# A fused two-block transformer on one core: each merge step carries an attention step, and seven stand between group norm steps

## The chip, the cores and the metric

The kernel runs on one core of a Trainium2 chip. The metric is the device time of one execution in microseconds (us), as the median of several runs. The engines are PE (TensorE, the matrix engine), DVE (VectorE), ACT (ScalarE), POOL (GpSimd) and SP (SyncE, which here issues the DMAs).

## The reference

Two transformer blocks on 256 tokens of width 1024, all in float32. Only block one matters here:

```python
def first_block(x, p, ...):
    u = rmsnorm(h, mix_pre_norm[i])
    z = u @ w_in[i]                                   # attention, RWKV and gate columns
    o_attn = dilated_attention_branch(z_attn)         # 4 heads, 3 dilation groups, 2 blocks of 128 queries
    o_rwkv = rwkv7_time_mix(z_rwkv, ...)              # 8 heads, a recurrence over the tokens, then group norm
    gate_attn, gate_rwkv = jnp.split(jax.nn.sigmoid(z_gate), 2, axis=-1)
    merged = gate_attn * (o_attn @ w_attn_up[i]) + gate_rwkv * (o_rwkv @ w_rwkv_up[i])
    h = h + rmsnorm(merged @ w_out[i], mix_post_norm[i])
    ...                                               # a feed-forward part and a gated embedding
```

Block two (three more attentions, an attention to a memory, a gated feed-forward part and the last norm) follows and is computed from `h`.

## The kernel before

Weights stream from DRAM through six slots of 1 MB. Each product with them is done in pieces (`parts` in the rows): a weight is split into a high part (ACT, a copy) and a low part (DVE, L2422), and PE multiplies high by high, high by low and low by high (L691, L692, L693).

The work is written as five programs, one for each engine, and all five walk through the same list of steps. A step is what stands between two `yield`s of a Python generator; the object `turns` says which generator gives the next step. Since an engine works its instructions off in the order in which they are written, the order of the steps is the order on every engine, and semaphores make one engine wait for another.

In the stretch of this case two generators are mixed (`turns.mix(fills(), rwkv(), order_1())`, L1309):

- "m", the fills. First the products for queries, keys and values, `qkv()`. Then the merge products (`gates()`: the 2048 gate columns of `w_in`, 4 ranges of 512 columns, 8 steps each, so 32 steps; a step is 6 matmuls of 128x512, called a gate step here) and `attention()` (24 steps). For each block of 128 queries i (0 or 1) and each pair of heads hh (0 or 1) the attention has 6 steps on PE: scores (L1231), nothing, transposes of one head (L697), transposes of the other (L697), nothing, values (L1274). In the first step DVE masks the scores of one head and takes their minimum (L2758), waits for ACT's exponential (L1694), inverts the sum (L2761) and scales (L2368, called the end of that head's softmax); in the second step it does the other head. For i=0 a head has 384 columns, for i=1 768. Then come the products with `w_attn_up` (two steps here, the rest later).
- "s", RWKV. For each chunk of 128 tokens i: products of keys and receptances, `first()` (L1053, L1068, L1081; DVE masks them at L2670 to L2673, L2678 and L2685), and `chain()`, six levels of a matrix inversion. A level is a step T (PE L1105 and L1108, then DVE masks the result, L2695, two instructions) and a step X (PE L1121 to L1129, then ACT copies it). After them come S (L1140; DVE copies it, L2701), X21 (L1150), the right side (L1171), u (L1185) and y (L1196 to L1201). `normed(i)` is the group norm of y: ACT copies y, DVE means and subtracts (L2640 to L2644), ACT squares, DVE sums (L2648), POOL takes the root (L3332), DVE scales (L2654), PE transposes (L697), ACT and DVE finish. The norm of chunk 0 runs beside the chain of chunk 1, the norm of chunk 1 after y. Then the four products with `w_rwkv_up` (L1288), beside which `w_out`'s first two slots are split.

How m and s alternate is a string written by hand, and how gates and attention alternate another:

```python
return itertools.chain("msmsm" * 12, "msmsmsm" * 16, "mmsmmsmsmsmsms", itertools.cycle("ms"))   # L532
yield from turns.alternate(gates(), attention(), "aab")                                          # L1304
```

With "aab" two gate steps are followed by one attention step; when the gates are at an end, the last 8 attention steps stand alone. Results go to 8 banks of PSUM. The attention takes banks 2, 3 and 4 in turn, RWKV banks 4, 5, 6 and 7, the gates banks 0 and 1: bank 4 has two owners. Before PE writes a bank again it waits until the engine that reads it has done so (`bank()`, which waits for the events in `free`).

Of the kernel before, what the change touches and what calls it, by code (L numbers as in the profile page):

```python
# [274 lines left out]
def program(nc, A, consts, vecs, pt, out):  # L275
    with ExitStack() as ctx:
# [54 lines left out]
        def const(off, n):  # L331
            return low[:, OC + off:OC + off + n]
# [196 lines left out]
              "wo2": (A["w_out_2"][0], [P + 26152, P + 28200, P + 19968, P + 17920], m2Hi, m2Lo)}  # L529

        def order_1():
            return itertools.chain("msmsm" * 12, "msmsmsm" * 16, "mmsmmsmsmsmsms", itertools.cycle("ms"))  # L532

# [142 lines left out]
        def tensor_program(e, turns):  # L678
# [4 lines left out]
            def bank(b):  # L683
                for event in free[b]:
                    q.wait_ge(*event)
                return PSUM[:, b, :]
# [254 lines left out]
            def gate(r, late):  # L941
                yield from token_range(st1, GATE_AT[r], 2, 512, lambda i: [main_act.at("g1", r, i)], late)

            def gates():
                for r in (2, 3, 0, 1):
                    yield from gate(r, (lambda: rotate("qk", 5, 2, rz1[1])) if r == 2 else nothing)
# [270 lines left out]
                yield from up("r", lambda k: ("rwkv_up", k), 4, o_rwkv, wait_rwkv, lambda i, n: [up_dve.at("r", i, n)], rw_bank)  # L1217

            def attention():
                for i in range(2):  # L1220
                    for hh in range(2):
                        W = 128 * (i + 1)
                        nb = 3 * (i + 1)
                        bs = [next(pa) for _ in range(i + 2)]
                        for b in bs:
                            bank(b)
                        q.wait_ge(*rope_dve.at("qk", 5, "sum"))

                        def score(par, g, b, o):
                            half = half_rows[par]  # L1230
                            return mm(PSUM[:, bs[b], o:o + W], qk[half, 2 * g + hh, 128 * i:128 * i + 128], qk[half, 6 + 2 * g + hh, 0:W], True, True)  # L1231

                        if i == 0:
                            for g in range(3):
                                for par in range(2):
                                    t = score(par, g, par, 128 * g)
                                    if g == 2:
                                        t.then_inc(at_pe.up("s", i, hh, par), 1)
                            for par in range(2):
                                free[bs[par]] = [at_dve.at("r", i, hh, par, 0)]  # L1240
                        else:
                            score(0, 2, 1, 0).then_inc(at_pe.up("shared", hh), 1)
                            for n in range(2):
                                t = score(0, n, 0, 256 * n)
                                if n == 1:
                                    t.then_inc(at_pe.up("s", i, hh, 0), 1)
                                score(1, 1 + n, 2, 256 * n)
                            q.wait_ge(*at_pe.at("shared", hh))
                            score(1, 0, 1, 256).then_inc(at_pe.up("s", i, hh, 1), 1)
                            for b, event in zip(bs, ((0, 0), (1, 0), (1, 1))):  # L1250
                                free[b] = [at_dve.at("r", i, hh, *event)]
                        yield
                        yield
                        for par in range(2):
                            q.wait_ge(*at_dve.at("e", i, hh, par))
                            for b0 in range(0, nb, 4):
                                k = min(4, nb - b0)
                                b = next(pa)
                                p = bank(b)
                                for j in range(k):  # L1260
                                    t = tr(p[:, 128 * j:128 * j + 128], at_sm[par][:, 128 * (b0 + j):128 * (b0 + j) + 128])
                                t.then_inc(at_pe.up("t", i, hh, par, b0), 1)
                                free[b] = [at_act.at("t", i, hh, par, b0)]
                            yield
                        yield
                        b = next(pa)
                        p = bank(b)
                        q.wait_ge(*main_act.at("v", 1, 1))
                        q.wait_ge(*at_act.at("t", i, hh, 1, 4 if nb > 4 else 0))
                        for n in range(nb):  # L1270
                            g, j = n // (i + 1), n % (i + 1)
                            for par in range(2):
                                h = 2 * hh + par
                                t = mm(p[half_rows[par], 0:128], vtok[:, j, 64 * (4 * g + h):64 * (4 * g + h) + 64],  # L1274
                                       at_eT[par][:, 128 * n:128 * n + 128], n == 0, n == nb - 1)
                        t.then_inc(at_pe.up("o", i, hh), 1)
                        free[b] = [at_act.at("o", i, hh)]
                        yield
# [22 lines left out]

            def fills():
                yield from qkv()
                yield from turns.alternate(gates(), attention(), "aab")  # L1304
                for _ in range(2):
                    turns.go("up", ups)
                    yield
# [376 lines left out]
        def scalar_program(e, turns):  # L1684
# [3 lines left out]
            def bank(b):  # L1688
                return PSUM[:, b, :]
# [172 lines left out]
            def gates():  # L1862
                for r in (2, 3, 0, 1):
                    yield from gate(r)
# [124 lines left out]
                yield from rwkv_up()  # L1989

            def attention():
                for i in range(2):
                    for hh in range(2):
                        W, nb = 128 * (i + 1), 3 * (i + 1)
                        for _ in range(i + 2):
                            next(pa)
                        for par in range(2):
                            q.wait_ge(*at_dve.at("r", i, hh, par, i))
                            s = at_sm[par][:, 0:3 * W]
                            act(s, s, ACT.Exp, scale=-1.0, bias=sm_at[par][0][:, i:i + 1], accum=sm_at[par][1]) \  # L2000
                                .then_inc(at_act.up("x", i, hh, par), 1)
                            yield
                        for par in range(2):
                            for b0 in range(0, nb, 4):
                                k = min(4, nb - b0)
                                p = bank(next(pa))
                                q.wait_ge(*at_pe.at("t", i, hh, par, b0))
                                copy(at_eT[par][:, 128 * b0:128 * (b0 + k)], p[:, 0:128 * k]).then_inc(at_act.up("t", i, hh, par, b0), 1)
                            yield
                        yield  # L2010
                        p = bank(next(pa))
                        q.wait_ge(*at_pe.at("o", i, hh))
                        copy(o_attn[:, hh, 128 * i:128 * i + 128], p[:, 0:128]).then_inc(at_act.up("o", i, hh), 1)
                        yield
# [15 lines left out]

            def fills():
                yield from qkv()
                yield from turns.alternate(gates(), attention(), "aab")
                for _ in range(2):
                    turns.go("up", ups)
                    yield
# [321 lines left out]
        def vector_program(e, turns):  # L2358
# [184 lines left out]
            def gates():  # L2543
                for r in (2, 3, 0, 1):
                    yield from gate(r, (lambda: rotate1(5)) if r == 2 else nothing)
# [189 lines left out]

            def attention():
                ma = const(C_MA, 768)
                for i in range(2):
                    for hh in range(2):
                        W, nb = 128 * (i + 1), 3 * (i + 1)  # L2740
# [53 lines left out]

            def fills():
                yield from qkv()
                yield from turns.alternate(gates(), attention(), "aab")
                for _ in range(2):
                    turns.go("up", ups)
                    yield  # L2800
# [427 lines left out]
        def gpsimd_program(e, turns):  # L3228
# [46 lines left out]
            def steps(n):  # L3275
                for _ in range(n):
                    yield
# [31 lines left out]
            def gates():  # L3309
                for r in (2, 3, 0, 1):  # L3310
                    yield from gate(r, nothing)
# [34 lines left out]
                yield from steps(4)  # L3346

            def attention():
                yield from steps(24)

            ups = steps(4)

            def fills():
                yield from qkv()
                yield from turns.alternate(gates(), attention(), "aab")
                for _ in range(2):
                    turns.go("up", ups)
                    yield
# [194 lines left out]
```

## Time and profile before

| | us |
|---|---|
| median of three runs | 983.81 (983.28 to 984.82) |
| the profiled execution, its own time | 984.61 |
| its span in the trace | 982.5 |
| PE busy in the span | 939.3 (96%) |
| DVE busy | 578.5 (59%) |
| ACT busy | 426.5 (43%) |
| mean granted clock of PE | 0.995 of full speed |

Times in rows are microseconds from the start of the span; "busy" of PE is modelled, since its matmuls are pipelined, so the time from the start of one piece to the start of the next is the better measure of a piece. The stretch of this case goes from 156 to 286 us. The masking instruction of the attention is called CUSTOM_DVE_ANT in the trace and ISA in the order of the program.

### The profile page before, as it was taken

To read this page: it belongs to the slowest core of one execution; us is meant where nothing else is said; L and a number is where in the kernel's file an instruction comes from. 1 tells how busy PE (TensorE), PEld (TensorE's weight loads), DVE (VectorE), ACT (ScalarE), POOL (GpSimd) and SP (SyncE) were. 2 spreads that over 40 slices of the span, in tenths; PEclk is the share of its full clock that TensorE was granted. 3 is DMA by queue.
4 is the path that set the end of the run, shared out by engine and by line. 5 is a ranking of instruction groups with operands and counts; after the bars stand their busy time and mean duration, and the time that the engine had idled before them with its cause. 6 is when DMAs were issued, how large, how long until landed. Compare 5 with 4: busy or idle time off the path is not lost.

```text
span 982.5 us, 15768 instructions
## 1 busy us (share of the span) xinstructions
PE 939.3 (96%) x6794; PEld 773.5 (79%) x6794; DVE 578.5 (59%) x903; ACT 426.5 (43%) x679; POOL 46.9 (5%) x62
## 2 busy tenths in 40 slices
PE   5999999989989999999999999989999899999996
PEld 3998888767558988888879988765568698888885
DVE  1569765744463566655764567853672456667672
ACT  2574334333342344455543446462430344455560
POOL 1010000100000000000000450000000000000000
PEclk9999999999999999999999999999999999999999
DMA  9345242221545865555438684323555457675531
GB/s 330 116 129 172 89 129 87 88 79 58 209 159 165 248 178 190 195 183 203 128 129 191 137 239 139 128 87 111 191 169 150 117 157 197 173 192 194 177 123 43
DMA packets 134948, 151.83 MB, mean 155 GB/s; under 512 B 15936, under 2 KB 106304, under 8 KB 134752
## 3 DMA queue, kind: packets, MB, share of 16 engines
q1 hardware_dynamic: 133952, 147.14, 48.5%
q10 hardware_dynamic: 928, 3.70, 1.0%
q8 instruction: 53, 0.87, 0.4%
q14 instruction: 15, 0.12, 0.0%
HBM read 149.78 MB, written 1.05 MB: 154 GB/s over the span
## 4 chain that ended last, share of the span: by engine, by line
PE 85%; DVE 7%; ACT 4%; issue 2%; DMA 1%; POOL 0%; POOLq 0%; SPq 0%; ACTq 0%; DVEq 0%
PE psum L802 10%; PE psum L691 8%; PE psum L693 8%; PE psum L692 8%; PE psum L754 7%; PE psum L803 6%; PE psum L774 4%; PE psum L1288 4%; PE psum L775 3%; PE psum L783 3%; PE psum L697 2%; PE psum L860 2%; PE psum L850 2%; PE psum L851 2%; PE psum L805 1%
## 5 line engine op out<-in xcount | busy, mean ns | idle before, releaser
L1697 ACT ACTIVATE parts<-low 128x1024 fp32r<-128x1024 f32 (+2 forms) x234 | 236.9, 1047 | 107.0 <-PE psum L693 64.1
L2422 DVE TENSOR_TENSOR parts<-low,parts 128x1024 fp32r<-128x1024 f32 (+2 forms) x148 | 181.1, 1251 | 39.7 <-ACT parts L1697 39.2
L691 PE MATMUL psum<-parts 128*128 128x512 f32 (+2 forms) x424 | 170.9, 403 | 2.7 <-DVE parts L2422 2.7
L693 PE MATMUL psum<-parts 128*128 128x512 f32 (+2 forms) x424 | 164.1, 387 | 0.0
L692 PE MATMUL psum<-parts 128*128 128x512 f32 (+2 forms) x424 | 163.8, 386 | 0.0
L802 PE MATMUL psum<-parts 128*128 128x512 f32 x434 | 155.7, 398 | 0.0
L1697 ACT ACTIVATE high<-psum 128x512 f32<-128x512 f32 (+5 forms) x103 | 56.5, 566 | 184.3 <-PE psum L805 73.0
L803 PE MATMUL psum<-parts 128*128 128x256 f32 x496 | 129.1, 281 | 0.0
L691 PEld LDWEIGHTS psum<-parts 128*128 128x128 f32 x424 | 79.8, 188 | 23.5 <-DVE parts L2422 4.9
L803 PEld LDWEIGHTS psum<-parts 128*128 128x128 f32 x496 | 93.6, 189 | 5.7
L802 PEld LDWEIGHTS psum<-parts 128*128 128x128 f32 x434 | 81.7, 188 | 16.9
L693 PEld LDWEIGHTS psum<-parts 128*128 128x128 f32 x424 | 79.8, 188 | 16.3
L692 PEld LDWEIGHTS psum<-parts 128*128 128x128 f32 x424 | 79.9, 188 | 15.2 <-issue 1.2
L2482 DVE TENSOR_TENSOR parts<-low,parts 128x1024 fp32r<-128x1024 f32 x54 | 66.0, 1222 | 35.3 <-ACT parts L1697 35.3
L774 PE MATMUL psum<-parts 128*128 128x256 f32 x280 | 74.3, 300 | 2.1 <-ACT parts L1697 2.1
L754 PE MATMUL psum<-low 128*128 128x128 f32 (+2 forms) x640 | 73.3, 275 | 2.4 <-DVE low L2399 2.4
L754 PEld LDWEIGHTS psum<-low 128*128 128x128 f32 (+2 forms) x640 | 71.9, 188 | 3.8 <-DVE low L2399 3.3
L775 PE MATMUL psum<-parts 128*128 128x256 f32 x280 | 69.3, 282 | 0.0
L774 PEld LDWEIGHTS psum<-parts 128*128 128x128 f32 x280 | 53.4, 191 | 6.5 <-issue 5.3
L775 PEld LDWEIGHTS psum<-parts 128*128 128x128 f32 x280 | 53.5, 191 | 1.3 <-issue 1.2
L2837 DVE TENSOR_TENSOR mid<-psum,high 128x512 f32<-128x512 f32 x31 | 21.4, 692 | 44.7 <-ACT high L1697 44.7
L3236 POOL TENSOR_TENSOR low<-low 128x1 f32<-128x1 f32 x20 | 11.0, 552 | 676.6 <-DVE low L2368 676.6
(304 smaller groups left out, 1330.9 us busy)
## 6 DMA issues: line engine op xcount, KB each, us to landing
low<-in_w_in_dram SPq DMA_DIRECT2D x40, 1024.0 KB, 5.2
low<-in_w_ffn_in_dram SPq DMA_DIRECT2D x44, 512.0 KB, 5.1
low<-in_w_ff_in_dram SPq DMA_DIRECT2D x16, 1024.0 KB, 5.8
low<-in_w_ff_out_dram SPq DMA_DIRECT2D x16, 1024.0 KB, 4.9
low<-in_w_ffn_out_dram SPq DMA_DIRECT2D x11, 1024.0 KB, 5.0
low<-in_w_out_dram SPq DMA_DIRECT2D x8, 1024.0 KB, 6.0
low<-in_w_ple_gate_dram SPq DMA_DIRECT2D x4, 1024.0 KB, 5.0
low<-in_w_up_dram SPq DMA_DIRECT2D x3, 1024.0 KB, 5.0
```

The source lines that it names most:

```text
L691: mm(o, l[0], r[0], start, False)
L692: mm(o, l[0], r[1], False, False)
L693: return mm(o, l[1], r[0], False, stop)
L754: t = mm(PSUM[0:m, banks[n], 256 * j + 128 * i:256 * j + 128 * i + 128], w3[:, k, off:off + m], uT[:, k, 128 * i:128 * i + 128], k == 0, k ...
L774: mm(o, hi[:, k, c], st.uh[:, k, :], k == 0, False)
L775: mm(o, lo_[:, k, c], st.uh[:, k, :], False, False)
L802: mm(p, hi[:, k, c], st.u2(k), k == 0, False)
L803: mm(p[:, 0:256], lo_[:, k, c], st.uh[:, k, :], False, False)
L1288: t = mm(p, l[:, k, 128 * i:128 * i + 128], slot(held(*key(k // 2)))[:, 1024 * (k % 2) + 512 * n:1024 * (k % 2) + 512 * n + 512], k == 0, ...
L1697: return e.activation(o, a, ACT.Copy)
L2422: tt(rslot3(n, nk, width)[:, r, 0:w], slot3(n, nk, width)[:, r, 0:w], st.hi3(j)[:, r, 0:w].bitcast(F32), ALU.subtract) \
L2482: tt(rview(OR + 2048 * n + 1024 * (k % 2), 1024), slot(n)[:, 1024 * (k % 2):1024 * (k % 2) + 1024], rview(base, 1024).bitcast(F32), ALU.su ...
```

## The change

Three things are changed, in all engine programs alike. `attention()` starts with an empty step, so it has 25. Gates and attention are no longer alternated by "aab" but paired: each m step is one gate step followed in the same step by one attention step, so that after 25 of the 32 steps the attention is at an end and seven gate steps are left. And the string of `order_1` is another: from the sixth group on it is written out, with one s between m and m nearly everywhere, twice two in a row ("mssmss"), and "sssss" at the end of the group norm.

```diff
-            return itertools.chain("msmsm" * 12, "msmsmsm" * 16, "mmsmmsmsmsmsms", itertools.cycle("ms"))
+            return itertools.chain("msmsm" * 12, "msmsmsm" * 5, "ms" * 7, "mssmss", "ms" * 23, "sssss", itertools.cycle("ms"))
@@ def attention(): (in each engine's program; POOL's has steps(25) for steps(24))
+                yield
                 for i in range(2):
                     for hh in range(2):
@@ def fills(): (in each engine's program)
                 yield from qkv()
-                yield from turns.alternate(gates(), attention(), "aab")
+                yield from turns.paired(gates(), attention())
                 for _ in range(2):
                     turns.go("up", ups)
                     yield
```

`turns.paired(a, b)` stands in the kernel already: each of its steps is a step of a and then one of b, while both last.

No instruction is added or removed on any engine; lines behind the new ones are two or three higher (DVE's L2695 is L2697 there, L2758 is L2761, L2422 is L2424; PE's L1288 is L1289). Three places show what moves.

The first is DVE in the third level of chunk 1's chain, before. L2758 to L2368 are one head of the attention for i=0 (384 columns), the two L2695 the masks of a step T, L2422 a split of the gate weights:

```order
L2758 ISA mid,low<-psum,low 128x384
L2758 ISA low 128x1
L2761 RECIPROCAL low<-low 128x1
L2368 TENSOR_SCALAR mid<-mid,low 128x384
L2695 TENSOR_TENSOR high<-psum,low 64x512 x2
L2422 TENSOR_TENSOR parts<-low,parts 128x1024
```

And the same place on DVE in the changed kernel (L2761 and L2764 are the attention, L2697 the masks, L2424 the split):

```order
L2761 ISA mid,low<-psum,low 128x512
L2761 ISA low 128x1
L2761 ISA mid,low<-psum,low 128x256
L2761 ISA low 128x1
L2764 RECIPROCAL low<-low 128x1
L2370 TENSOR_SCALAR mid<-mid,low 128x768
L2697 TENSOR_TENSOR high<-psum,low 64x512 x2
L2424 TENSOR_TENSOR parts<-low,parts 128x1024
L2761 ISA mid,low<-psum,low 128x256
```

The head ahead of the masks is now one of i=1, with 768 columns in two pieces, and the next head's first piece stands right behind the split. In the sixth level the same stands once more, without the split.

The second is DVE at the start of chunk 1, in the changed kernel: masks of the key products (L2672 to L2675, the last three rows of six are shown), the mean of the group norm, the masks L2680 and L2687, with an attention head between them:

```order
L2675 TENSOR_TENSOR high<-high,low 128x4x64
L2642 TENSOR_REDUCE low<-high 128x8
L2370 TENSOR_SCALAR low<-low 128x8
L2646 TENSOR_TENSOR high<-high,low 128x512
L2680 TENSOR_TENSOR high<-psum,low 128x4x128 x2
L2761 ISA mid,low<-psum,low 128x384
L2761 ISA low 128x1
L2764 RECIPROCAL low<-low 128x1
L2370 TENSOR_SCALAR mid<-mid,low 128x384
L2687 TENSOR_TENSOR high<-psum,low 128x512 x2
```

Before, L2685 (the same as L2687) followed L2678 (L2680) at once, and no attention head stood ahead of the six masks either.

The third is PE at the end of the stretch, before: L1288 are the products with `w_rwkv_up` and `w_attn_up`, L1231, L697 and L1274 the attention's scores, transposes and values:

```order
L697 MATMUL psum<-low,mid 128x128 x6
L1288 MATMUL psum<-low,high 128x512 x4
L1274 MATMUL psum<-mid 64x128 x12
L1288 MATMUL psum<-low,high 128x512 x4
L1231 MATMUL psum<-mid 128x256 x6
L1288 MATMUL psum<-low,high 128x512 x8
L697 MATMUL psum<-low,mid 128x128 x12
L1274 MATMUL psum<-mid 64x128 x12
L1288 MATMUL psum<-low,high 128x512 x8
L697 MATMUL psum<-low,high 128x128 x8
```

The same place on PE in the changed kernel, from the last gate matmul on:

```order
L693 MATMUL psum<-parts 128x512
L697 MATMUL psum<-low,high 128x128 x4
L1289 MATMUL psum<-low,high 128x512 x24
L697 MATMUL psum<-low,high 128x128 x8
L850 MATMUL psum<-parts 128x512
```

The attention is gone from there: all of it stands between gate steps and RWKV's steps, up to the step u of chunk 1. Between y and the transposes of the group norm stand six gate steps and nothing else.

## Rows read from the trace of the kernel before

**Rows 1.** The page, the chain that ended last, by engine:

```profile
PE 85%; DVE 7%; ACT 4%; issue 2%; DMA 1%; POOL 0%; POOLq 0%; SPq 0%; ACTq 0%; DVEq 0%
```

**Rows 2.** Waits of PE, 155 to 290 us: total, times, longest:

```profile
PE psum L1121 <- DVE high L2695: 3.2, 4, 1.1
PE psum L697 <- DVE mid L2368: 2.0, 1, 2.0
PE psum L1105 <- ACT high L1697: 1.0, 1, 1.0
PE psum L697 <- ACT mid L1697: 0.9, 1, 0.9
PE psum L1274 <- DVE high L2371: 0.8, 1, 0.8
PE psum L697 <- DVE high L2654: 0.8, 1, 0.8
PE psum L1274 <- ACT mid L1697: 0.7, 1, 0.7
PE psum L1288 <- issue: 0.4, 1, 0.4
```

**Rows 3.** Timeline of PE, end of the stretch: start, length, work, idle before:

```profile
256.56 1.53 PE L1274 MATMUL psum<-mid 128*64 128x128 f32 x24 [0.78 <-DVE high L2371]
...
275.70 2.83 PE L1274 MATMUL psum<-mid 128*64 128x128 f32 x24 [0.69 <-ACT mid L1697]
```

**Rows 4.** Windows: busy of PE, PEld, DVE, ACT, POOL, granted clock, DMA, GB/s:

```profile
275.00:276.00 1.00, 0.31 (x5) 0.33 (x6) 0.86 (x1) 0.56 (x2) 0.00 (x0) 0.72 0.99 408
...
647.00:648.00 1.00, 1.00 (x4) 0.80 (x5) 1.00 (x7) 1.00 (x3) 0.00 (x0) 0.75 0.08 16
```

**Rows 5.** Waits of PE, 640 to 655 us, in block two:

```profile
PE psum L691 <- DVE parts L2422: 1.8, 1, 1.8
```

**Rows 6.** Timeline of DVE: a head of the attention for i=1:

```profile
240.87 0.69 DVE L2758 CUSTOM_DVE_ANT_0 mid<-psum,low 128x512 f32<-128x512 f32 x1 [0.76 <-PE psum L1231]
...
243.39 0.62 DVE L2368 TENSOR_SCALAR mid<-mid,low 128x768 f32<-128x768 f32 x1
```

**Rows 7.** Timeline of DVE: a head for i=0, T's masks, a split:

```profile
197.75 0.56 DVE L2758 CUSTOM_DVE_ANT_1 mid<-psum,low 128x384 f32<-128x384 f32 x1 [1.21 <-PE psum L1231]
...
199.62 1.40 DVE L2695 TENSOR_TENSOR high<-psum,low 64x512 f32<-64x512 f32 x2
201.05 1.23 DVE L2422 TENSOR_TENSOR parts<-low,parts 128x1024 fp32r<-128x1024 f32 x1
```

**Rows 8.** Timeline of PE: first matmuls of a T, the gate step, the X:

```profile
197.64 0.27 PE L1105 MATMUL psum<-high 64*64 64x64 f32 x1
...
198.72 0.50 PE L691 MATMUL psum<-parts 128*128 128x512 f32 x1
...
201.17 0.24 PE L1121 MATMUL psum<-high 64*64 64x64 f32 x1 [0.78 <-DVE high L2695]
```

**Rows 9.** Timeline of DVE: chunk 1's masks and the group norm between:

```profile
176.65 0.42 DVE L2670 TENSOR_TENSOR high<-psum,low 128x256 f32<-128x256 f32 x1 [0.52 <-PE psum L1056]
...
180.93 1.29 DVE L2678 TENSOR_TENSOR high<-psum,low 128x512 f32<-128x512 f32 x2
182.26 1.29 DVE L2685 TENSOR_TENSOR high<-psum,low 128x512 f32<-128x512 f32 x2
```

**Rows 10.** Timeline of ACT: an exponential for i=0, and the next work:

```profile
198.34 0.61 ACT L1694 ACTIVATE mid<-mid,low 128x384 f32<-128x384 f32 x1 [1.02 <-DVE low L2758]
...
198.96 0.58 ACT L1693 ACTIVATE mid<-psum 128x512 f32<-128x512 f32 x1
```

**Rows 11.** Timeline of PE: four gate steps in a row, from first to next:

```profile
240.87 0.50 PE L691 MATMUL psum<-parts 128*128 128x512 f32 x1
...
246.69 0.81 PE L697 MATMUL psum<-low,mid 128*128 128x128 f32 x6
```

**Rows 12.** Timeline of POOL, the root of chunk 1's group norm:

```profile
246.02 1.64 POOL L3332 TENSOR_TENSOR low<-low 128x8 f32<-128x8 f32 x1 [59.04 <-DVE low L2368]
```

More of the change, by code:

```diff
@@ L1991, in attention @@
             def attention():
+                yield
                 for i in range(2):
@@ L2032, in fills @@
                 yield from qkv()
-                yield from turns.alternate(gates(), attention(), "aab")
+                yield from turns.paired(gates(), attention())
                 for _ in range(2):
@@ L2737, in attention @@
                 ma = const(C_MA, 768)
+                yield
                 for i in range(2):
@@ L2796, in fills @@
                 yield from qkv()
-                yield from turns.alternate(gates(), attention(), "aab")
+                yield from turns.paired(gates(), attention())
                 for _ in range(2):
@@ L3348, in attention @@
             def attention():
-                yield from steps(24)
+                yield from steps(25)
             ups = steps(4)
@@ L3354, in fills @@
                 yield from qkv()
-                yield from turns.alternate(gates(), attention(), "aab")
+                yield from turns.paired(gates(), attention())
                 for _ in range(2):
```

## The prediction, made before the changed kernel ran

> **What bounds the kernel now.** The page's chain that ended last comes first: PE holds 85% of it, DVE 7%, ACT 4% [rows 1]. So the kernel is PE's queue plus the places where PE waits, and the change adds and removes no instruction: it can only move those waits, and what the clock does behind them. The waits of PE between 155 and 290 us are the second view: 9.8 us [rows 2]. They are of two kinds. In the chain of chunk 1 PE waits at X for T's masks on DVE and once at T for ACT's copy: 3.2 + 1.0 = 4.2 us. At the end of the stretch, where attention steps stand without a gate step beside them, it waits 2.0 + 0.9 + 0.8 + 0.8 + 0.7 + 0.4 = 5.6 us. Third, the timeline there: the same 24 matmuls of the values take 1.53 us once and 2.83 us the second time, 1.3 us more [rows 3]; the window shows a granted clock of 0.72 where they begin [rows 4], a mean over part of a microsecond at each of the levels 2.4 and 1.2 GHz. PE had waited 2.0, 0.9 and 0.7 us just before.
>
> **What the change takes away.** All attention leaves the end of the stretch. Three of its waits (2.0, 0.9, 0.7) were attention's own; the 0.8 at L1274 was for a bank that the values shared with the read of an RWKV product, and both are apart now. The 0.8 at the norm's transposes came from two heads queued on DVE within the norm; now ACT and DVE have nothing there but two splits ahead of it, and six gate steps cover it: four take 246.69 - 240.87 = 5.8 us [rows 11], so six 8.7 us, while the norm takes about 6.5 us (POOL 1.64 [rows 12], some 4.9 for eight pieces on ACT and DVE, estimated from 0.58 for a copy [rows 10] and 0.7 for a mask [rows 7]). Cover is left for 2 us. The 0.4 ahead of L1288 I leave standing: PE now does 24 of these products in a row, and DVE's two splits can hold up their reads about as much. With the 1.3 us of the slow clock: 5.2 + 1.3 = 6.5 us gone. The 4.2 us in the chain go too, since an m step is a gate step and mostly an attention step now, and are counted anew below. Together 10.7 us.
>
> **What it puts in.** The unit is a level of the chain. From T to what follows it PE needs 198.72 - 197.64 = 1.1 us, a gate step 1.6 (PE was free at 201.17 - 0.78 = 200.39); X starts 0.15 us after the two masks, which take 1.4 [rows 7, 8]. So T, gate step, X just fits if DVE is free. It is not when a head of the attention stands ahead of the masks: a head for i=0 holds DVE from 197.75 to 199.62, 1.9 us, and that made the 0.8 us before this X [rows 7, 8]. A head for i=1 holds it from 240.87 to 243.39 + 0.62, 3.1 us, of which it sleeps about 1.1 on ACT's exponential, masks queued behind [rows 6]. Before, no head for i=1 stood in the chain. Now two first heads do, in its third and sixth levels.
> - Third level: from the end of the scores DVE needs 3.1 (head) + 1.4 (masks) + 1.2 (split) + 0.45 (the next head's first piece: 0.56 for 384 columns, here 256) + 0.15 = 6.3 us, and X must wait for that last piece too, since it writes bank 4, where those scores lie. PE has T and one gate step, 2.7 us. Wait 3.6.
> - Sixth level: 3.1 + 1.4 + about 1.3 (both pieces of the next head, bank 4 again) + 0.15 = 5.95, less 2.7: 3.25.
> - Start of chunk 1 ("mssmss": only three gate steps where six stood). ACT copies y, whose bank PE needs next, behind an exponential: 0.6 + 0.6 + 0.6 + 0.15 less a product of 1.1: 0.9 [rows 10]. Then DVE's six masks and the norm's mean take 180.93 - 176.65 = 4.3 us and the next masks 1.3 [rows 9], against LR 1.1, gate step 1.6, M 1.05 on PE, and the second M needs their bank: 1.9. Then DVE has a head 2.2, masks 1.3, sums 0.8, masks 1.3, a split 1.2 and T's masks 1.4, 8.1 us with the 0.15, against M, gate step, transposes, T, gate step, transposes, 6.15 on PE: 1.95.
> - End of chunk 0: DVE copies S behind a head, a split and a second head (0.5 + 1.9 + 1.2 + 1.9 + 0.7 + 0.15 = 6.4) against 5.7 on PE: 0.7. X of the fifth level waits for the copy of the values out of bank 4, 0.5.
> Sum 3.6 + 3.25 + 0.9 + 1.9 + 1.95 + 0.7 + 0.5 = 12.8 us.
>
> The Trainium skill says in Perfetto Trace Analysis, section Matmuls, that independent matmul groups should rotate through different PSUM banks, so that reading one overlaps with the next group's matmuls. Were attention and RWKV on different banks, the third level's wait would be 3.6 - 1.2 - 0.45 = 1.95 us and the sixth's 1.95; no run here has shown that.
>
> **The clock** is the one price that the trace shows only elsewhere. After 2.0, 0.9 and 0.7 us of waits it fell at 275 us; at 647 us it fell to 0.75 within a microsecond after a single wait of 1.8 us [rows 4, 5]. After single waits of up to 1.1 us in the chain it did not. Waits of 3.6 and 3.25 us in one piece lie well above both cases, so I let it fall after each. A fall costs between nothing (if it runs out while PE waits) and what halving costs the work behind it; the nearest row is 1.3 us [rows 3], and I take that twice: 2.6.
>
> **The sum** is made against the profiled execution, 984.61 us (span 982.5 and 2.1 around it): -10.7 + 12.8 + 2.6 = +4.7, 989.3 us. The median of the runs lies 0.8 below that execution, so 988.5 for the median. Behind the stretch all is moved as one: the last `w_out` slot is asked for when the products with `w_rwkv_up` end and is needed after those with `w_attn_up` and their transposes, over 7 us later instead of 15; I count nothing for it, and up to 1 us if that load is late.
>
> **The rivals.** The unknown is what a wait that stands in no row of before costs.
> - *No fall of the clock.* The waits are as counted, PE's clock stays at 2.4 GHz: +2.1, median 985.9. For it: the chain kept its clock through four waits in 20 us. Against it: the one wait of 1.8 us at 647. Chance 0.2.
> - *A third fall*, in the start of chunk 1, where 1.9 and 1.95 us of waits lie within ten: +6.0, median 989.8. A wait of 1.8 did it once, the small matmuls around this one may matter. Chance 0.15.
> - *The long heads are not paid in full* (this one ends faster). One mechanism: PE does not stand still behind the heads for i=1, so third and sixth level cost what an i=0 head costs, 0.8 each, and the clock never falls: -10.7 + 12.8 - 6.85 + 1.6 = -3.15, median 980.7. It decides once these two levels cost together less than about 2.8 us, since all other terms sum to -4.8 and 2 us is what a measurement can tell. For it: 1.1 us of a head are sleep, in which a queue that was not strict would work, and the copies of S and y may find gaps. Against it: in the chain a head of 1.9 us was paid to the last tenth. Chance 0.12.
> - That the change does not do what it says can be left out: its order has the steps as told.
>
> The Trainium skill's section Optimization Strategy of Perfetto Trace Analysis says that stretches bound by different engines may gain when they are interleaved. That is the case for the last rival: the end was bound by DVE and ACT, the gate steps by PE. The rows agree for the end, 6.5 us, and speak against it in the chain, which had less room on DVE than PE's busy share tells.
>
> **Chances.** The forecast, 988.5, has 0.53. About 0.2% (2 us) is what a measurement of this kernel tells from no change: faster means under 981.8, slower over 985.8. Faster: 0.10, nearly all of the last rival. Same: half of the case without a fall, the rest of the last rival and forecasts whose waits are 3 us too large, 0.20. Slower: 0.70. The range, 983.5 to 991.0, takes in both clock cases, a start of chunk 1 that costs 2 us less, and leaves out the faster case and a little above; the forecast's own range is 986.5 to 990.5.
>
> **What would show it.** In the profile of the changed kernel: no attention line (L1232, L1275) behind y, and PE without a wait over 0.5 us from the last gate step to L850; two waits at L1121 of 3 us or more, released by DVE's L2761, with the attention head of 768 columns and L2697 right before on DVE; a wait of about 2 us at L1081, released by L2680; a granted clock under 1 behind the two long waits and at 1.00 where the values of before were slow. The forecast is wrong if the waits at L1121 sum to under 4 us, or if the stretch from the first scores to L850 is not longer than before.

## The result, and the profile after

The changed kernel takes 988.96 us (median of four executions, 987.49 to 989.81) against 984.32 for the kernel before on the same chip (983.28 to 985.36). The ratio is 1.004, with a 95% interval of 1.0026 to 1.0053: slower, by 4.6 us. The profiled execution took 989.52 us, its span is 987.3, 4.8 more than before, and the mean granted clock 0.989 against 0.995.

The page's chain that ended last, by engine, reads almost as before [rows 1]:

```profile
PE 85%; DVE 8%; ACT 3%; issue 2%; DMA 1%; POOL 0%; POOLq 0%; SPq 0%; ACTq 0%; DVEq 0%
```

The waits of PE from 155 to 295 us in the changed kernel (total, times, longest), which answer to [rows 2]:

```profile
PE psum L1121 <- DVE low L2761: 6.5, 2, 3.5
PE psum L1081 <- DVE high L2680: 1.9, 1, 1.9
PE psum L1068 <- ACT high L1698: 0.8, 1, 0.8
PE psum L1150 <- DVE high L2703: 0.7, 1, 0.7
PE psum L1121 <- ACT mid L1698: 0.6, 1, 0.6
PE psum L1121 <- ACT high L1698: 0.4, 1, 0.4
PE psum L850 <- ACT parts L1694: 0.3, 1, 0.3
PE psum L1289 <- DVE mid L2373: 0.2, 1, 0.2
```

Of the eight waits of [rows 2] only the one at L1288 is left, 0.2 us at L1289. In their place stand two long ones at X, in the third and the sixth level, and five shorter ones. The 0.3 us at L850 stand in the trace of the kernel before as well, so I count them on neither side: 11.1 us now against 9.8. The timeline of PE (start, length, work, idle before) gives their places:

```profile
187.81 1.60 PE L1081 MATMUL psum<-high 64*128 64x256 f32 x8 [1.92 <-DVE high L2680]
...
195.99 0.27 PE L1121 MATMUL psum<-low,high 64*64 64x64 f32 x1 [0.58 <-ACT mid L1698]
...
213.04 0.37 PE L1121 MATMUL psum<-high 64*64 64x64 f32 x1 [3.50 <-DVE low L2761]
...
239.72 0.36 PE L1121 MATMUL psum<-high 64*64 64x64 f32 x1 [3.04 <-DVE low L2761]
...
269.29 0.60 PE L697 MATMUL psum<-low,high 128*128 128x128 f32 x4
269.73 17.33 PE L1289 MATMUL psum<-low,high 128*128 128x512 f32 x40
```

The last two rows are the end of the stretch: the norm's transposes at 269.29 follow the last gate step without a wait, and the products of L1289 stand in one piece.

DVE ahead of the third level's X, in the same columns; it answers to [rows 6, 7]:

```profile
206.81 0.69 DVE L2761 CUSTOM_DVE_ANT_0 mid<-psum,low 128x512 f32<-128x512 f32 x1 [2.58 <-PE psum L1232]
...
207.54 0.48 DVE L2761 CUSTOM_DVE_ANT_0 mid<-psum,low 128x256 f32<-128x256 f32 x1
...
209.13 0.16 DVE L2764 RECIPROCAL low<-low 128x1 f32<-128x1 f32 x1 [1.10 <-ACT mid L1695]
209.33 0.62 DVE L2370 TENSOR_SCALAR mid<-mid,low 128x768 f32<-128x768 f32 x1
209.86 1.40 DVE L2697 TENSOR_TENSOR high<-psum,low 64x512 f32<-64x512 f32 x2
211.30 1.23 DVE L2424 TENSOR_TENSOR parts<-low,parts 128x1024 fp32r<-128x1024 f32 x1
212.56 0.42 DVE L2761 CUSTOM_DVE_ANT_0 mid<-psum,low 128x256 f32<-128x256 f32 x1
```

DVE sleeps 1.10 us on the exponential while T's masks (209.86) are queued behind, though PE has written what they read by 207.96; and the piece that frees bank 4 (212.56) comes after the split. From 206.81 to X at 213.04 it is 6.23 us.

The windows of the changed kernel (busy shares, and third from the end the granted clock), which answer to [rows 4]:

```profile
188.00:189.00 1.00, 1.00 (x8) 0.69 (x7) 0.14 (x2) 1.00 (x4) 0.00 (x0) 0.68 0.00 0
189.00:190.00 1.00, 1.00 (x4) 0.56 (x3) 0.90 (x3) 0.98 (x2) 0.00 (x0) 0.50 0.00 0
...
212.00:213.00 1.00, 0.00 (x0) 0.00 (x0) 0.96 (x3) 0.00 (x0) 0.00 (x0) 0.62 0.00 0
213.00:214.00 1.00, 0.96 (x36) 0.96 (x40) 0.76 (x2) 0.18 (x1) 0.00 (x0) 0.50 0.00 0
...
218.00:219.00 1.00, 1.00 (x6) 0.76 (x4) 0.00 (x0) 0.22 (x1) 0.00 (x0) 0.50 0.09 12
219.00:220.00 1.00, 1.00 (x31) 0.91 (x32) 0.00 (x0) 1.00 (x3) 0.00 (x0) 0.96 0.87 123
...
239.00:240.00 1.00, 0.28 (x9) 0.28 (x11) 0.66 (x2) 0.30 (x1) 0.00 (x0) 0.78 0.00 0
240.00:241.00 1.00, 1.00 (x36) 1.00 (x35) 0.21 (x2) 0.73 (x2) 0.00 (x0) 0.50 0.00 0
...
243.00:244.00 1.00, 1.00 (x7) 0.80 (x6) 0.00 (x0) 1.00 (x2) 0.00 (x0) 1.00 0.00 0
```

The clock stood at 1.2 GHz (0.50) three times in the stretch: at 188 to 192 us, at 212 to 219 and at 239 to 243. A gate step in the second of these, on PE:

```profile
214.96 0.79 PE L691 MATMUL psum<-parts 128*128 128x512 f32 x1
...
217.68 0.63 PE L697 MATMUL psum<-low,mid 128*128 128x128 f32 x2
```

2.72 us from the step's start to the next work, where it is 1.6 at full clock.

### The profile page after: what moved, and what is told of

Its sections match the earlier page's. It is cut to its first block, busy times and chain, and to the rows that moved or that the text cites. A ratio compares the mean times of both kernels' runs of the same rounds, so it can differ in the third digit from the quotient of the medians.

```text
span 987.3 us, 15764 instructions
## 1 busy us (share of the span) xinstructions
PE 943.0 (96%) x6794; PEld 777.6 (79%) x6794; DVE 578.3 (59%) x903; ACT 427.8 (43%) x679; POOL 46.1 (5%) x62
## 4 chain that ended last, share of the span: by engine, by line
PE 85%; DVE 8%; ACT 3%; issue 2%; DMA 1%; POOL 0%; POOLq 0%; SPq 0%; ACTq 0%; DVEq 0%
PE psum L802 10%; PE psum L691 9%; PE psum L692 8%; PE psum L693 8%; PE psum L754 7%; PE psum L803 6%; PE psum L774 4%; PE psum L1289 4%; PE psum L775 3%; PE psum L783 3%; PE psum L697 3%; PE psum L860 2%; PE psum L850 2%; PE psum L851 2%; DVE parts L2424 1%
## 5 line engine op out<-in xcount | busy, mean ns | idle before, releaser
L2424 DVE TENSOR_TENSOR parts<-low,parts 128x1024 fp32r<-128x1024 f32 (+2 forms) x148 | 181.2, 1252 | 37.3 <-ACT parts L1698 36.8
L691 PE MATMUL psum<-parts 128*128 128x512 f32 (+2 forms) x424 | 172.4, 407 | 2.8 <-DVE parts L2424 2.8
L691 PEld LDWEIGHTS psum<-parts 128*128 128x128 f32 x424 | 80.5, 190 | 23.7 <-DVE parts L2424 4.5
```

The source lines that it names most:

```text
L691: mm(o, l[0], r[0], start, False)
L2424: tt(rslot3(n, nk, width)[:, r, 0:w], slot3(n, nk, width)[:, r, 0:w], st.hi3(j)[:, r, 0:w].bitcast(F32), ALU.subtract) \
```

## The experiments

Each ratio is against the kernel before, run on the same chip beside it (its median was 984.5 in the first group of four, 984.9 in the other two); the changed kernel's is 1.004. Where an edit adds lines, those behind it have higher numbers in its rows (the L1121, L2761 and L2680 of the changed kernel are L1125, L2765 and L2684 in e_fill). "The stretch" of a trace is the time from the first gate step behind 155 us to the first L850: 131.05 us before (156.21 to 287.26), 135.36 in the changed kernel (156.83 to 292.19).

**e_fill**: the holes filled. In PE's step X of chunk 1, ahead of the wait:

```diff
+    if i == 1:
+        oB = bank(bs[1])
+        for _ in range({2: 4, 5: 3}.get(lv, 0)):
+            mm(oB, const(C_ID, 128), const(C_M0, 512), True, True)
```

> The changed kernel with matmuls that nothing reads (128x512, a constant by itself, into a bank that the next step overwrites) put ahead of X in the third level (4 of them) and the sixth level (3) of chunk 1's chain, where PE stands still for 3.50 and 3.04 us. PE has work in both holes and waits only for their rest. The result is the same. Forecast (the clock falls after a long wait, and costs 1.3 us each): the holes are no longer than before, since PE does nothing useful in them, the clock stays at 2.4 GHz from 209 to 243 us, and the time is 2.6 us under the changed kernel, about 986.4. Reading of the changed kernel's trace (the slow clock costs 2.8 and 1.3 us there): 4.1 us under it, about 984.9. Rival, the low clock belongs to the small matmuls behind the holes and not to the holes: it falls all the same, same time as the changed kernel or up to 1 us more, 989 to 990.

984.01 us, ratio 0.9993 (0.9984 to 1.0003): 4.6 under the changed kernel by the ratios, more than either size expected. In its trace no window of the stretch is under full clock. Of the windows and waits (PE, 155 to 295 us) of e_fill:

```profile
213.00:214.00 1.00, 1.00 (x42) 0.89 (x33) 0.13 (x2) 0.83 (x1) 0.00 (x0) 1.00 0.09 16
```

```profile
PE psum L1081 <- DVE high L2684: 1.9, 1, 1.9
PE psum L1125 <- DVE high L2701: 1.4, 1, 1.4
PE psum L1125 <- DVE low L2765: 0.5, 1, 0.5
```

The two X start no earlier than in the changed kernel (5.15 and 4.69 us behind the start of the gate step ahead of them, against 5.15 and 4.70): the holes are as long, only filled, all but 0.5 us. Work that nobody reads makes the kernel as fast as the one before: the slow clock is the whole net loss. The first X of chunk 1 waits 1.4 here instead of 0.58: in the changed kernel slow PE work covers part of that wait. The stretch takes 130.69 us, 4.7 less than in the changed kernel. The clock also stayed up behind the 1.90 us at L1081 (187.69 us), where the edit puts nothing; that part of the gain, some 0.5 us net, is not the edit's by any row here.

**e_fill3** (only `{2: 4}`) and **e_fill6** (only `{5: 3}`):

> The changed kernel with unread matmuls only in the hole of the third level (4, as in e_fill). By the trace of the changed kernel the slow clock there cost 2.8 us and that of the sixth level 1.3; the forecast had 1.3 each. Trace: 2.8 under the changed kernel, 986.2. Forecast: 1.3 under it, 987.7. Rival, the length of a slow stretch is chance and not the place's: the sixth level's is then as often long, and this gives about 2, 987.

> The changed kernel with unread matmuls only in the hole of the sixth level (3, as in e_fill). Trace: 1.3 under the changed kernel, 987.7. Forecast: the same. Rival, as in e_fill3: about 2, 987.

985.51 us, ratio 1.0000 (0.9991 to 1.0008), and 987.00 us, ratio 1.0020 (1.0011 to 1.0029): 3.9 and 2.0 under the changed kernel. The order is the one of the trace's reading, both are larger than it; their sum, 5.9, lies over the 4.6 of both together, by about as much as four executions of the changed kernel leave open (1.3 either way). The traces are closer to the reading. The stretch is 133.99 us in e_fill6, 1.4 under the changed kernel, and 131.27 in e_fill3, 4.1 under it. In the trace of e_fill3 the wait of the sixth level is 3.0 as before, but no slow clock came behind it, so its 4.1 hold the third level's 2.7 and the sixth's 1.4. The forecast's equal 1.3 is out for the third level.

**e_minima**: on DVE both heads' minima first, both heads' ends a step later.

```diff
                                 ...
+                        yield
+                        for par in range(2):
+                            sm = at_sm[par]
+                            nm, den, rden = sm_at[par]
                             q.wait_ge(*at_act.at("x", i, hh, par))
                             ...
-                            yield
+                        yield
```

> The changed kernel, but DVE masks the scores and takes the minimum for both heads in the first step after the scores, and inverts and scales both in the next step. T's masks no longer stand behind DVE's sleep on the exponential, and bank 4 is read out one step earlier. Forecast's theory (DVE in the order of its queue ahead of T's masks makes the waits of the third and sixth level): third level's wait = four pieces of the masking 2.3 + masks 1.4 + 0.15 less T and gate step 2.7, about 1.2 instead of 3.50; sixth the same, 1.2 instead of 3.04; the clock does not fall in either: 4.1 from the waits and 4.1 from the clock less, some of it given back as both heads' ends come later (up to 1): about 981, under the kernel before. Rival, PE waits at X for something else than DVE's queue (the bank alone, or the exponential): waits stay over 2.5 each and the time within 1 us of the changed kernel, 989.

978.14 us, ratio 0.994 (0.9926 to 0.9955), 9.8 under the changed kernel; expected were 8. PE's waits at X and at L1081 in this trace:

```profile
PE psum L1121 <- DVE high L2697: 3.6, 3, 1.4
PE psum L1081 <- DVE high L2680: 1.1, 1, 1.1
```

The third and sixth level wait 1.09 and 1.10 us where 1.2 was expected, the releaser is now T's masks, and the clock stays at full in the whole stretch. So what stands on DVE ahead of the masks and ahead of the read of bank 4 made the long waits. The edit moves three things at once: the sleep of 1.10 us, the end of the first head, and the read of the next head's first piece, which comes ahead of the masks now; e_banks below takes the last by itself.

**e_before_minima**: the same edit on the kernel before.

> The same edit of DVE's attention steps on the kernel before. The waits in its chain at L1121 (3.2 us in four) lose the sleep on the exponential, some 0.6 each where a head for i=0 stands ahead, but get a second head's minimum instead of the end of the first; at the end of the stretch the transposes wait for the first head about 1 us longer each time. Forecast's theory: within 1 us of the kernel before, 983.5 to 985.5: the sleep is short beside what the move puts in. Rival: the edit is a gain wherever it stands (the sleep is what costs), 2 us or more under the kernel before, 982 or less; then a gain in the changed kernel would say little on its long heads.

977.58 us, ratio 0.9931 (0.9918 to 0.9944). I was wrong by 6 us: the rival holds. Its waits of PE from 155 to 295 us, to be read against [rows 2]:

```profile
PE psum L1121 <- DVE high L2695: 2.5, 3, 1.1
PE psum L1274 <- DVE high L2371: 0.8, 1, 0.8
PE psum L1274 <- ACT mid L1697: 0.7, 1, 0.7
PE psum L1288 <- issue: 0.4, 1, 0.4
PE psum L697 <- DVE mid L2368: 0.3, 1, 0.3
PE psum L850 <- ACT parts L1693: 0.3, 1, 0.3
```

The 2.0 at the transposes is 0.3, the waits for ACT at T and at the transposes (1.0, 0.9) and the norm's 0.8 are gone, and with them the slow clock at 275. The sleep cost the kernel before as well, mostly at its end, and there more than in the chain where I looked. With the edit in both, the reordering is worth nothing: 978.14 against 977.58, with overlapping intervals. And since the edit gains 6.8 us without any long head in the chain, the 9.8 us of e_minima say little on those heads, as the rival had it; what shows them are the waits at X, 3.50 and 3.04 us against 1.09 and 1.10.

**e_banks**: the attention's banks in another turn, on PE, ACT and DVE.

```diff
-            pa, pg = itertools.cycle((2, 3, 4)), itertools.cycle((0, 1))
+            pa, pg = itertools.cycle((3, 4, 2)), itertools.cycle((0, 1))
```

> The changed kernel with the attention's three banks taken in the turn 3, 4, 2 instead of 2, 3, 4, on PE, ACT and DVE. In the third level of chunk 1's chain the X then no longer writes the bank in which the next head's scores lie, and waits only for T's masks: 3.50 less the split 1.23 and the piece 0.42 is 1.95 by the prediction's sum. In the sixth level bank 4 holds the first piece of the next head only: about 0.8 of the 3.04 less. Theory of the forecast: waits of about 1.9 and 2.2, clock still falls after the longer one or both; 2.4 us of waits less plus 0 to 4.1 of clock: 982.5 to 986.5, likeliest 985.5. Rival, the bank is not what holds X (it is the masks, and the bank comes free no later): waits stay over 3, time as the changed kernel, 989. Another level may collide in place of these, which would show as a new wait at L1121 or L1274.

985.72 us, ratio 1.0011 (1.0002 to 1.002), as expected. PE's waits:

```profile
PE psum L1121 <- DVE low L2761: 2.2, 1, 2.2
PE psum L1081 <- DVE high L2680: 1.9, 1, 1.9
PE psum L1121 <- DVE high L2697: 1.9, 1, 1.9
PE psum L697 <- DVE high L2687: 0.9, 1, 0.9
```

The third level waits 1.87 for the masks alone; the sixth 2.24, for the piece in bank 4. So 1.6 of the 3.50 was the shared bank. The clock fell behind the waits of 1.90 and 1.87, for 1.7 us each, and not behind that of 2.24.

**e_ms**: plain alternation at the start of chunk 1.

```diff
-   "msmsmsm" * 5, "ms" * 7, "mssmss", "ms" * 23, "sssss", ...
+   "msmsmsm" * 5, "ms" * 32, "s" * 7, ...
```

> The changed kernel with a plain alternation at the start of chunk 1: "ms" 32 times and seven s, instead of "ms" 7 times, "mssmss", "ms" 23 times and five s. Six gate steps stand there again where three stood, and the group norm of chunk 1 gets four gate steps instead of six; the attention comes a level earlier, so the long heads stand in the second and fifth level. By the prediction's terms: 0.9 + 1.9 + 1.95 less, norm 6.5 against 5.8 of cover 0.7 more: 4.05 under the changed kernel, 984.9. By the waits of the changed kernel's trace (0.8 + 1.9 + 0.6, and some 0.5 net of a slow clock at 188 to 192 us, less 0.7): 3.1 under it, 985.9. Both: two waits near 3 us at L1121 with the clock falling behind them stay. Rival, the waits of that place only move on to the next levels, since DVE is what is short there: 988 to 989.

992.03 us, ratio 1.0063 (1.0046 to 1.0081), 2.3 us over the changed kernel, where both theories and the rival had it faster or the same. The intervals of the two just overlap, but the stretch in the trace is longer too, 137.71 us against 135.36. DVE in the second level of e_ms:

```profile
205.61 1.40 DVE L2697 TENSOR_TENSOR high<-psum,low 64x512 f32<-64x512 f32 x2
207.04 0.69 DVE L2662 TENSOR_TENSOR high<-high 128x512 f32<-128x512 f32 x1
207.77 0.69 DVE L2664 TENSOR_TENSOR high<-high 128x512 f32<-128x512 f32 x1
208.38 1.22 DVE L2424 TENSOR_TENSOR parts<-low,parts 128x1024 fp32r<-128x1024 f32 x1
209.63 0.42 DVE L2761 CUSTOM_DVE_ANT_0 mid<-psum,low 128x256 f32<-128x256 f32 x1
```

One level earlier the long head meets two instructions that finish chunk 0's group norm (L2662, L2664), and X waits 4.83 us, 1.3 more than the 3.50 of the changed kernel; the two instructions take 1.4. The waits of the start did shrink (0.8, 1.9 and 0.6 became 1.1 and 0.6), but the slow clock lasted long behind both long waits. The step that I overlooked is that a shift of the attention moves it past the other DVE work too.

**e_minima_ms**: both edits.

> The plain alternation of e_ms and the DVE edit of e_minima in one kernel. If the two terms are separate, the start of chunk 1 gives the 1.1 and 0.8 us that still stand at L1081 and L1068 in e_minima, less 0.7 for the norm: 978.1 - 1.2 = 976.9. Rival, they share a cause (DVE's heads): nothing left to give, and the norm's 0.7 more: 978.8.

980.39 us, ratio 0.9947 (0.9933 to 0.9962): no gain over e_minima, nearer to the rival. The norm's transposes wait 0.8 with four gate steps ahead of them, as the prediction had it (6.5 against 5.8).

**e_stag_banks** and **e_stag_before**: heads staggered on DVE, the first with the banks of e_banks on the changed kernel, the second on the kernel before.

```diff
                                 ...
-                            q.wait_ge(*at_act.at("x", i, hh, par))
-                            ...
+                            if par == 1:
+                                end(0)
                             yield
+                        end(1)
```

> The changed kernel; on DVE the heads are staggered (first step after the scores: minimum of head 0; second: minimum of head 1 and end of head 0; third: end of head 1), so that no sleep and only one head's minimum, 1.15 us, stands ahead of T's masks, and the attention's banks in the turn 3, 4, 2. Theory of the forecast (what stands on DVE ahead of the masks, and the bank, make the wait): third level 1.15 + 1.4 + 0.15 - 2.7 = 0, sixth with the next head's first piece (bank 4) 0.7, no fall of the clock behind them: 2.5 us under e_minima, about 975.6. Rival, the minimum of two heads in e_minima was free beside other work, or the bank turn brings new waits at the transposes (0.9 and 0.4 stood there with this turn): 977.5 to 979.

> The kernel before, with the heads staggered on DVE in the same way and the banks as they were. Against the edit e_before_minima (977.6) the T masks stand behind one minimum of 0.56 instead of two: up to 0.6 us less at each of three levels, and no transposes wait for a sleep: 976. Rival, the end of head 0 behind the second minimum now delays other work of DVE as much: same as e_before_minima, 977.6.

e_stag_banks: 977.46 us, ratio 0.9923 (0.991 to 0.9937), with no slow clock in its trace but the one at the kernel's end, which all fourteen traces have. The third level no longer waits, the sixth 0.4; but transposes wait 1.3 and 0.4 for ACT's copies and 1.5 at the start of chunk 1, as its rival said. e_stag_before: 985.86 us, ratio 1.0009 (0.9998 to 1.0019): no gain, though e_before_minima gained 6.8. Its wait at the end, where the attention has no gate steps beside it:

```profile
PE psum L697 <- DVE mid L2368: 5.0, 2, 3.5
```

An end put off by a step lands behind w_out's splits on DVE there, 2.36 us, and PE stands 3.5 us; the slow clock behind it is a long one. DVE sleeps on no exponential at that place, so where a head's end comes in the queue costs as much as the sleep did.

**e_before_fill**: the two holes ahead of the last transposes of before filled.

```diff
+    if (i, hh) == (1, 1):
+        b = next(pa)
+        p = bank(b)
+        for _ in range(2 - par):
+            mm(p, const(C_ID, 128), const(C_M0, 512), True, True)
     q.wait_ge(*at_dve.at("e", i, hh, par))
```

> The kernel before with unread matmuls (128x512, two and one, into the bank that the transposes then overwrite) in the two holes ahead of the last head's transposes, where it waits 2.0 and 0.9 us and where the clock falls behind. This sizes the term of 1.3 us that the prediction removed with the end of the stretch. Forecast: 1.3 under the kernel before, 983.2. Reading with the long slow stretches that other kernels show: up to 2.8 under, 981.7. Rival, the clock there costs nothing net since DVE is what is late behind it: the same as before.

982.19 us, ratio 0.9974 (0.9964 to 0.9983): 2.6 us. The slow clock at 275 is gone, and the stretch in the trace takes 129.69 us, 1.4 less than before: the forecast's 1.3. In seven of nine executions the mean clock is 0.998, as in the traces whose only slow stretch is the one at the kernel's end, so the one at 647 us, far behind the edit, was mostly gone as well; the rest of the 2.6 is most likely its share, which no run takes apart.

**e_mix**: e_minima's steps for i=0, e_stag_banks' for i=1, the banks turned from i=1 on (of the edit only the last is shown).

```diff
                 for i in range(2):
+                    if i == 1:
+                        next(pa)
```

> A kernel put together from what has been seen: the changed kernel; on DVE both heads' minima in one step for i=0 (as e_minima), heads staggered for i=1 (as e_stag_banks), and the attention's banks turned by one from i=1 on alone, so that the banks at the start of chunk 1 stay as they were. Expected: the waits of third to sixth level as in e_stag_banks (1.1 in all instead of 4), those of the start as in e_minima (1.1 and 0.8, without the 1.5 and 1.3 at the transposes): 2.9 us under e_minima, 975.2, under both kernels and all variants. Rival, the transposes of the staggered heads wait as they did in e_stag_banks (1.3 of its 1.7 belong to them and not to the start): 976.5 to 978.

978.67 us, ratio 0.9934 (0.9921 to 0.9946): the rival. Of its waits:

```profile
PE psum L697 <- ACT high L1700: 1.7, 2, 1.3
PE psum L1121 <- DVE high L2701: 1.4, 1, 1.4
PE psum L1081 <- DVE high L2684: 1.1, 1, 1.1
```

The third and sixth level gave their 1.1 and 0.7, but the transposes wait 1.7 and the X of the fourth level 0.74, while the fifth lost its 0.38. Five versions (e_stag_banks, e_before_minima, e_mix, e_minima, e_minima_ms) are faster than both kernels by 0.5 to 0.8% of the kernel before; these runs do not tell which of them is best.

## Why the prediction was right, and where it was not

- **The sign and the size.** Forecast 988.5, measured 988.96; +4.7 forecast against the profiled execution, +4.9 measured (989.52 - 984.61). But the size is right partly by luck, since errors cancel. Net of what goes, the forecast had +3.4 us for the waits (12.8 - 9.4) and +1.3 for the clock (2.6 - 1.3), and nothing for PE's own work; the trace has +1.3, +4.3 and -1.3. Neither of the two signs that would have made the forecast wrong came: the waits at L1121 released by L2761 are 6.5 us, and the stretch is longer.
- **What goes, 10.7.** Confirmed: the waits of before are gone, six gate steps (260.97 to 269.29, 8.3 us where I had 8.7) cover the norm, and the 0.4 that I left standing is 0.2.
- **Third and sixth level, 3.6 and 3.25.** Measured 3.50 and 3.04. The mechanism is shown from three sides: with the sleep and the head's end behind the masks, and bank 4 read ahead of them, 1.1 each (e_minima), without the shared bank 1.87 in the third (e_banks, for which the prediction had 1.95), and in e_ms other DVE work in the same place adds to the wait.
- **Start of chunk 1, 0.9 + 1.9 + 1.95.** The first two are 0.80 and 1.92. The third is 0.58 and so the mis-sized wait. Where the clock stays up it is 1.5 (0.16 + 1.38 in e_fill); the other 1.0 is covered in the changed kernel by PE's slow work. The working of this term has a slip too: its seven numbers and the 0.15 add up to 8.35, not 8.1, so by its own terms the wait was 2.2.
- **End of chunk 0, 0.7 + 0.5.** 0.71 and 0.38. The new waits are 10.9 in all, forecast 12.8.
- **The clock, 2 x 1.3 = 2.6.** The term that was too small. In the profiled execution the clock fell three times, as the rival with the third fall had it, and one slow stretch was twice as long. From X to the next level's T, third level, PE needs 219.10 - 213.04 = 6.06 us against 3.34 in e_fill; from the sixth level's X to S 4.74 against 3.33; from the second product of L1081 (the prediction's second M) to T, the wait aside, 4.54 against 3.05. That is 2.7 + 1.4 + 1.5 = 5.6 us of PE's time, of which the 1.0 of covered wait comes back: 4.6 or 4.7, as e_fill measured. Taken together: waits 10.9 + 0.2 against 9.8, clock 5.6 against 1.3, makes +5.6; the stretch grew by 4.3 (131.05 to 135.36). The other 1.3 us are PE's own pieces, which took less in the new order; e_minima and e_before_minima show nearly the same, 1.0 (118.3 and 119.3 us of the stretch without its waits, neither with a slow clock). I had not foreseen it and no run takes it apart.
- **The rivals.** "No fall" would be 985.9; e_fill, which holds the clock up, gives 984.0, so the waits alone would have made no measurable change. "The long heads are not paid" is refuted by the 3.50 and 3.04. "A third fall" happened in the profiled execution; two of the other three have the same mean clock, 0.989, which does not tell where it fell. Its 989.8 lies 0.8 off the measured median and the forecast 0.5, so the times do not tell the two apart. I gave it 0.15, too little after a wait of 1.9 us when the only row like it, 1.8 us, had shown a fall.

The Trainium skill's rule on rotating PSUM banks (Perfetto Trace Analysis, section Matmuls) agrees with e_banks: 1.6 us of the third level's wait went when the two owners of bank 4 were apart there. The Trainium skill's advice that interleaving stretches of different bounds may help (Perfetto Trace Analysis, section Optimization Strategy) is borne out neither way: the end gained, the chain lost more (4.6 us net), and with the edit of e_minima in both kernels the interleaving is neutral.

## What to carry to other kernels

DVE worked its queue off in order here, through a sleep of 1.10 us with ready masks behind it. So before work is moved beside a dependent chain, add up on the other engine what will stand ahead of the chain's own instruction, a sleep on a third engine included, and try to take that sleep out first; here that gave 6.8 us in the kernel before, and the reordering nothing on top of it. But look where the put-off work lands: with one head's end put off by one step more (e_stag_before), the same was worth nothing. When PE must stand still for microseconds, price the clock behind the hole, not only the hole. And a shift by one step moves the work past everything else in the queue, so list what it meets there.

## What the runs showed of the hardware

All fourteen traces (both kernels and twelve experiments) have a slow stretch that begins in the last 3 to 6 us of the span and runs past its end; it is left out here (PE has started its last matmul 4 us earlier in the kernel before, at 974.36 against 978). The others came in two sizes. Summed over windows of 1 us, what the granted clock was short of full is 1.7 us in 16 of these 21 slow stretches and 3.4 in the other five. The five stand behind waits of 3.50, 3.49, 4.83, 3.04 and 3.53 us, the 16 behind shorter ones and once behind 3.04. Whether it falls is not settled by the wait alone: behind the same wait of 1.8 us in block two (L691 for DVE's split), with the same work around it, it fell in 8 of the 14 traces and stayed up in 6. Behind 1.9 us at L1081 it fell in four of the five traces that have that wait, and behind 3.02 us in e_fill3 and 2.24 us in e_banks it did not fall. The spread of a kernel's executions goes with the number of falls: e_before_fill takes 981.7 to 982.7 at a mean clock of 0.998 and 984.4 to 984.7 at 0.996; e_stag_banks, 0.998 in all five, takes 977.39 to 977.76.

Matmuls whose result nobody reads, put into the two holes of the changed kernel, went with a clock of 2.4 GHz through the whole stretch and gave back 4.6 us.
